# The second memory tile goes from the router's stage into the first pairs of experts, the first one is split, and the results of the memory products are stored once behind the experts

## The chip, the cores and the metric

One Trainium2 chip; the program runs on one of its cores. The metric is the device time of one execution in microseconds (us). TensorE (PE in the rows) has a clock of two levels, 1.2 and 2.4 GHz, and the profile gives the granted mean as a share of the upper one (PEclk).

## The reference

256 tokens (x) of width 1024 go through two blocks. The first adds an attention and mLSTM mix to x, and then a mixture of experts: 32 experts, of which each token uses two of one group. The second block has two layers (GLA and S5), and each layer also reads a memory of 256 rows, `mem_n`, by cross attention. All is in float32.

```python
h2 = modulate(x, norm2_g[l], sh2, sc2)
moe = hier_moe(h2.reshape(b * s, d), w_rg[l], b_rg[l], w_re[l], b_re[l],
               w1[l], w3[l], w2[l]).reshape(b, s, d)
x = x + g2[:, None, :] * moe
...
def memory_attention(q, mem_n, w_kv):
    k, v = jnp.split(mem_n @ w_kv, 2, axis=-1)
```

`mem_n @ w_kv` hangs on nothing in the first block, once the memory is normed. For the GLA layer its weights are four tiles: M0 and M1 give the keys (kept in `kmT`), M2 and a fourth one the values (kept in `vm`). For the S5 layer the keys and values are twelve quarters of a tile and more (`mem_quarters`, 0 to 3 keys, 4 to 11 values), whose results go to a tensor in the chip's memory, `s5_kv`, and are read back near the end.

## The kernel before

The kernel is written engine by engine, with semaphores set by hand. Weights come as tiles of 128 x 4096 floats (2 MB) from SP's queue into a ring of three slots (`k.ring`). The tuple FRONT is the order of the first 24 tiles: tile n goes to slot n % 3, its load waits until tile n - 3 is used (`tile_done`), and TensorE waits until it has landed (`landed`). M means a memory tile, A a tile of the modulation (`w_ada`), O one of the mix's output projection.

Each stage is a block of its own, with a barrier of all engines at its end:

- `stage_mix` ends with O0 and O1; SP loads the tiles up to M1 there, and the first two tiles of expert 0.
- `stage_route` scales x by its norm (`xn`), turns it (`turn`), makes `hT` from it on VectorE (`h_ready`), multiplies by the router's weights, and ranks the tokens of each expert. TensorE's queue holds M1, the turning, A10, the first half of M2 (M20), the router, a row of A10, turning h back, the second half (M21), A11 and the ranks, in this order. SP loads A10, M2, the third tile of expert 0, the first quarter, A11, `norm_f`, and then the three tiles of expert 1, which take the ring's slots as A10, M2 and A11 leave them.
- `stage_experts` works through 16 pairs of experts. The even ones of a pair have three buffers (`expert0`), the odd ones the three ring slots; SP loads each tile for the next pair when TensorE is done with the one in its place. In the first 12 pairs TensorE also multiplies one quarter with the turned memory (`memory_part`); ScalarE copies the result out of PSUM, and issues its store of 128 KB to `s5_kv` on its own queue. SP loads the next quarter between the even and the odd expert's tiles.
- `stage_first_end` adds the experts' sum to x, norms it, and multiplies the fourth memory tile, whose load SP has issued at the experts' end.

The GLA and S5 stages follow; the change does not touch them but for a wait on the ring that goes through `wait_tile`.

Of the kernel before, what the change touches and what calls it, by code (L numbers as in the profile page):

```python
# [15 lines left out]
P = 128  # L16
TOK = 256
TT = TOK // P
D = 1024
KD = D // P  # L20
# [3 lines left out]
RING = 3  # L24
TILE = 4096
# [9 lines left out]
         "O0", "O1", "M1", "A10", "M2", "A11")  # L35
# [11 lines left out]
N_QUARTER = 12  # L47
# [37 lines left out]
class Core:  # L85
# [59 lines left out]
    def wait_tile(self, pe, n):  # L145

        pe.wait_ge(self.landed[n % RING], 16 * (n // RING + 1))
# [108 lines left out]
def half_tile(k, banks, pe, p, kind, src):  # L256
# [3 lines left out]
    pe.wait_ge(*banks.free(p))  # L260
# [13 lines left out]
def ada_tile(k, banks, pe, m, crep):  # L274

    p = f"A{m}"
# [8 lines left out]
    last.then_inc(banks.done(p), 1)  # L285
# [660 lines left out]
def stage_route(k, a):  # L946

    with ExitStack() as ctx:
# [14 lines left out]
        banks = TwoBanks(k, "route", "M10:act M11:act A10:act M20:act G10:dve M21:act A11:act G11:dve")  # L963
# [5 lines left out]
        with k.nc.Block() as block:  # L969
            @block.sync  # L970
            def _(sp):
# [21 lines left out]
            def _(pe):  # L993
                k.wait_tile(pe, TILE_OF["M1"])
                for h in range(2):
                    out = banks.bank(f"M1{h}").rearrange("p (f t) -> p f t", f=2)
                    for f in range(2):
                        for kk in range(KD):
                            last = pe.matmul(out[:, f, :], k.slot(TILE_OF["M1"])[:, kk, (2 * h + f) * P:(2 * h + f + 1) * P],
                                             k.memT[:, kk, :], start=(kk == 0), stop=(kk == KD - 1))  # L1000
                    last.then_inc(banks.done(f"M1{h}"), 1)
# [3 lines left out]
                half_tile(k, banks, pe, "M20", "tm", k.memT)  # L1005
# [13 lines left out]
                half_tile(k, banks, pe, "M21", "tm", k.memT)  # L1019
# [26 lines left out]
            def _(act):  # L1046
# [10 lines left out]
                take("M11", a["kmT"][:, 6:8, :])  # L1057
                take("A10", a["part"][:])
                take("M20", a["vm"][:, 0, 0:512])
# [7 lines left out]
                take("M21", a["vm"][:, 1, 0:512])  # L1067
# [94 lines left out]
def stage_experts(k, a):  # L1162
# [7 lines left out]
    with ExitStack() as ctx:  # L1170
# [29 lines left out]
        with k.nc.Block() as block:  # L1200
            @block.sync
            def _(sp):
# [7 lines left out]
                def load_pair(p, i, off, part):  # L1210

                    for b in range(2):
# [3 lines left out]
                        if part and b == 0:  # L1216
                            sp.wait_ge(part_taken, p * N_QUARTER + i + (off + 1))
                            sp.dma_start(part_w[:].rearrange("p k n -> p (k n)"),
                                         k.dram["mem_quarters"][bass.ds(i + (off + 1), 1)].rearrange("a p n -> (a p) n")
                                         ).then_inc(part_in, 16)  # L1220

                with sp.Fori(0, n_pass) as p:
                    for off, count, part in ((0, N_QUARTER - 1, True), (N_QUARTER - 1, N_PAIR - N_QUARTER, False)):
                        with sp.Fori(0, count) as i:
                            load_pair(p, i, off, part)
                    with sp.If(p < n_pass - 1):
                        sp.dma_start(part_w[:].rearrange("p k n -> p (k n)"), k.dram["mem_quarters"][0]).then_inc(part_in, 16)
# [8 lines left out]
            def _(pe):  # L1236
# [22 lines left out]
                def memory_part(n, part):  # L1259
                    pe.wait_ge(part_in, n * 16)  # L1260
# [1721 lines left out]
```

## Time and profile before

| | before |
|---|---|
| time, median of 3 runs | 1515.02 us (1512.16 to 1519.53) |
| the profiled execution: time | 1515.57 us |
| its span, first to last instruction | 1513.8 us |
| TensorE matmuls busy | 1345.4 us (89%) |
| TensorE weight loads busy | 994.4 us (66%) |
| VectorE busy | 660.8 us (44%) |
| ScalarE busy | 264.6 us (17%) |
| GpSimd busy | 184.2 us (12%) |
| queue of SP, share of 16 DMA engines | 63.2%, 379.78 MB |
| queue of ScalarE | 1.3%, 6.88 MB |

The shares are means over stages with different limits. What a change in one stage is worth is read from that stage: the time line, the waits, and the windows, which give the busy time of each engine and the DMA traffic for a stretch. The route stage runs from 223.5 to about 266 us, the expert stage to about 742 us, and the stage behind it to 761.6 us.

### The profile page before, as it was taken

How to read it: one execution, taken by the hardware profiler on the slowest of the kernel's cores; microseconds unless marked ns; L12 is line 12 of the kernel's file. 1: busy time of each engine (PE TensorE's matmuls, PEld its weight loads, DVE VectorE, ACT ScalarE, POOL GpSimd, SP SyncE). 2: the span in 40 equal slices, each digit the busy share in tenths (PEclk: the TensorE clock that was granted, in tenths of full speed). 3: DMA queues.
4: the chain of work that ended last, by engine and by line, in shares of the span. 5: the costliest groups of instructions: out<-in, count | busy, mean ns of one | idle time of the engine just before them, and what ended most of it. 6: DMA issues, size and time to landing. Idle time of an engine off the chain costs nothing. (4 is left out here: it accounts for less than half of the span.)

```text
span 1513.8 us, 24904 instructions
## 1 busy us (share of the span) xinstructions
PE 1345.4 (89%) x10281; PEld 994.4 (66%) x10281; DVE 660.8 (44%) x1300; ACT 264.6 (17%) x555; POOL 184.2 (12%) x159
## 2 busy tenths in 40 slices
PE   5999989977677867766899999999999999999998
PEld 2475746544455544433458778888878878888887
DVE  2544334211101101110354326366399999886573
ACT  2212101111001100110211022100233323330000
POOL 0000010000000000000157550079300000000000
PEclk9999999998978898898899999999999999999999
DMA  9645737999999999999734334456564444334441
GB/s 401 231 159 224 283 124 319 398 428 428 426 428 428 427 428 428 428 427 429 339 131 167 112 113 165 158 176 227 201 206 160 157 163 137 146 112 152 157 176 45
DMA packets 50104, 387.67 MB, mean 256 GB/s; under 512 B 6368, under 2 KB 21472, under 8 KB 28144
## 3 DMA queue, kind: packets, MB, share of 16 engines
q1 hardware_dynamic: 45712, 379.78, 63.2%
q10 hardware_dynamic: 4320, 6.88, 1.3%
q8 instruction: 51, 0.84, 0.2%
q14 instruction: 21, 0.17, 0.0%
HBM read 379.76 MB, written 6.88 MB: 255 GB/s over the span
## 5 line engine op out<-in xcount | busy, mean ns | idle before, releaser
L2467 PE MATMUL ps<-hT,ring 128*128 128x256 f32 x768 | 174.5, 388 | 1.0 <-PEq L1910 1.0
L2467 PEld LDWEIGHTS ps<-hT,ring 128*128 128x128 f32 x768 | 148.8, 196 | 22.1 <-issue 1.4
L1390 DVE TENSOR_TENSOR act_slots<-gate,ps 64x256 f32<-64x256 f32 x32 | 13.5, 423 | 312.7 <-ACT gate L1337 312.7
L1285 PE MATMUL ps<-expert,x_gathered 128*32 128x256 f32 x1024 | 76.9, 453 | 66.0 <-DMA expert<-in_experts 64.9
L1285 PEld LDWEIGHTS ps<-expert,x_gathered 128*32 128x32 f32 x1024 | 34.6, 124 | 104.0 <-DMA expert<-in_experts 79.6
L1285 PE MATMUL ps<-ring,x_gathered 128*32 128x256 f32 x1024 | 64.8, 405 | 16.9 <-DMA ring<-in_experts 16.9
L1267 PE MATMUL ps<-mem_quarter,memT 128*128 128x128 f32 x256 | 48.2, 375 | 27.0 <-DMA mem_quarter<-in_mem_quarters 27.0
L264 PE MATMUL ps<-ring,hT 128*128 128x512 f32 x160 | 69.8, 593 | 0.0
L1267 PEld LDWEIGHTS ps<-mem_quarter,memT 128*128 128x128 f32 x256 | 46.7, 286 | 33.2 <-DMA mem_quarter<-in_mem_quarters 33.2
L1759 PE MATMUL ps<-ring,zT 128*128 128x256 f32 x288 | 66.8, 379 | 0.0
L1450 POOL TENSOR_SCALAR end_stat<-end_ss 128x1 f32<-128x1 f32 x2 | 0.9, 470 | 519.7 <-ACT expert L1440 519.6
L1285 PEld LDWEIGHTS ps<-ring,x_gathered 128*32 128x32 f32 x1024 | 35.1, 115 | 43.8 <-issue 13.1
L1367 DVE TENSOR_SCALAR sel_weighted<-const,rank,comb 128x128 f32<-128x128 f32 x66 | 19.8, 343 | 90.9 <-PE ps L1250 89.4
L1759 PEld LDWEIGHTS ps<-ring,zT 128*128 128x128 f32 x288 | 54.5, 190 | 7.4
L1953 PE MATMUL ps<-hT,ring 128*128 128x256 f32 x256 | 55.7, 379 | 0.0
L264 PEld LDWEIGHTS ps<-ring,hT 128*128 128x128 f32 x160 | 29.9, 190 | 35.8 <-issue 35.8
L1953 PEld LDWEIGHTS ps<-hT,ring 128*128 128x128 f32 x256 | 48.5, 190 | 6.5
L1255 PE MATMUL ps<-y,selT 32*128 32x256 f32 x528 | 48.4, 438 | 0.5 <-ACT y L1343 0.5
L1813 POOL TENSOR_SCALAR s_out_rstd<-s_out_ss 128x2 f32<-128x2 f32 x1 | 0.4, 368 | 398.5 <-ACT s_out_sq L1806 398.5
L1337 ACT ACTIVATE gate<-ps 64x256 f32<-64x256 f32 x32 | 12.1, 377 | 200.1 <-PE ps L1285 200.1
L283 PE MATMUL ps<-ring,crep 128*32 128x512 f32 x192 | 24.8, 637 | 12.4 <-DMA ring<-in_weights 12.4
L1664 PE MATMUL ps<-ring,hT 128*128 128x256 f32 x144 | 34.5, 382 | 0.0
(651 smaller groups left out, 2486.5 us busy)
## 6 DMA issues: line engine op xcount, KB each, us to landing
ring<-in_weights SPq DMA_DIRECT2D x72, 2048.0 KB, 8.3
expert<-in_experts SPq DMA_DIRECT2D x48, 2048.0 KB, 26.7
ring<-in_experts SPq DMA_DIRECT2D x48, 2048.0 KB, 26.7
mem_quarter<-in_mem_quarters SPq DMA_DIRECT2D x12, 512.0 KB, 20.1
s_c_bar<-c_bar_out ACTq DMA_DIRECT2D x16, 256.0 KB, 2.4
c_bar<-s_c_bar SPq DMA_DIRECT2D x16, 256.0 KB, 2.7
b_raw<-in_s_b SPq DMA_DIRECT2D x16, 128.0 KB, 7.2
s_a_rows<-s_ab_rows SPq DMA_DIRECT2D x64, 32.0 KB, 6.5
```

What stands on the lines that cost most here:

```text
L264: last = pe.matmul(bank, src[:, kk, h * P:(h + 1) * P], w[:, kk, :], start=(kk == 0), stop=(kk == KD - 1))
L283: last = pe.matmul(bank[32 * j:32 * j + 32, :], crep[:, 2 * j + i, :], w[:, 2 * j + i, :], start=(i == 0), stop=(i == 1), skip_group_check ...
L1255: last = pe.matmul(acc(g, t), selT[group(g), b, t * P:(t + 1) * P], y[group(g), :], start=False, stop=stop, skip_group_check=True)
L1267: last = pe.matmul(part_ps[:, h * P:(h + 1) * P], k.memT[:, kk, h * P:(h + 1) * P], part_w[:, kk, :], start=(kk == 0), stop=(kk == KD - 1))
L1285: last = pe.matmul(h_ps[group(g), :], xg[:, f, group(b)], w[:, kk, g, :], start=(f == 0), stop=(f == KD - 1))
L1337: act.activation(gate[:], h_ps[w1_out, :], ACT.Silu).then_inc(silu_done, 1)
L1367: last = dve.tensor_scalar(selw[:, b, t, :], k.c("iota32"), a["rank"][:, t, e], a["comb"][:, t, e], ALU.is_equal, ALU.mult)
L1390: dve.tensor_tensor(act_s[:], gate[:], h_ps[w3_out, :], ALU.mult).then_inc(act_ready, 1)
L1664: last = pe.matmul(self.ps(bank, h), rows[:, kk, :], w[:, kk, :], start=(start and h == 0 and kk == 0), stop=(kk == 3), skip_group_check=True)
L1759: last = pe.matmul(self.sum_of(n, p), rows[:, kk, :], w[:, kk, :], start=(first and kk == 0 and self.PLACE[p][1] == 0), stop=(self.ends(i) ...
L1953: last = pe.matmul(bank[:, f, :], w[:, kk, (2 * h + f) * P:(2 * h + f + 1) * P], k.hT[:, kk, :], start=(kk == 0), stop=(kk == KD - 1))
L2467: last = pe.matmul(out[:, f, :], w[:, kk, (2 * h + f) * P:(2 * h + f + 1) * P], k.hT[:, kk, :], start=(kk == 0), stop=(kk == KD - 1))
```

## The change

M2 leaves the ring. It gets a buffer of its own, `mem_tile`, loaded in the route stage, and is multiplied in four parts of 128 columns in pairs 0 to 3. The quarters move from pairs 0 to 11 to pairs 4 to 15. Their results are copied into `mem_tile`, whose weights are used by then, and one DMA in `stage_first_end` stores all twelve. M1 is multiplied in two halves: the first ahead of the turning, the second in M21's place. In FRONT M1 goes behind A10, and M2 to the end; A11 raises `tile_done` by two in M2's stead.

```diff
-         "O0", "O1", "M1", "A10", "M2", "A11")
+         "O0", "O1", "A10", "M1", "A11", "M2")
...
-        pe.wait_ge(self.landed[n % RING], 16 * (n // RING + 1))
+        outside = TILE_OF["M2"]
+        pe.wait_ge(self.landed[n % RING], 16 * (n // RING + 1 - int(n > outside and n % RING == outside % RING)))
...
-    last.then_inc(banks.done(p), 1)
+    last.then_inc(banks.done(p), 2 if m == 11 else 1)
...
-        banks = TwoBanks(k, "route", "M10:act M11:act A10:act M20:act G10:dve M21:act A11:act G11:dve")
+        banks = TwoBanks(k, "route", "M10:act A10:act G10:dve M11:act A11:act G11:dve")
...
-                tile(TILE_OF["A10"])
-                tile(TILE_OF["M2"])
+                tile(TILE_OF["A11"])
                 load_expert(k, sp, a, 0, 2)
+                sp.dma_start(a["mem_tile"][:], k.dram["weights"][TILE_OF["M2"]]).then_inc(a["mem_tile_in"], 16)
+                at = ROWS["norm_f_g"][0]
+                sp.dma_start(a["norm_f"][:], k.dram["rows"][at:at + D].partition_broadcast(P)).then_inc(norm_f_in, 16)
+                for n in ("A10", "M1", "A11"):
+                    sp.wait_ge(k.tile_done, TILE_OF[n] + 1)
+                    load_expert(k, sp, a, 1, TILE_OF[n] % RING)
                 sp.dma_start(a["mem_quarter"][:].rearrange("p k n -> p (k n)"), k.dram["mem_quarters"][0]
                              ).then_inc(a["mem_quarter_in"], 16)
-                tile(TILE_OF["A11"])
-                at = ROWS["norm_f_g"][0]
-                sp.dma_start(a["norm_f"][:], k.dram["rows"][at:at + D].partition_broadcast(P)).then_inc(norm_f_in, 16)
-                for n in range(T_END_FIRST - RING, T_END_FIRST):
-                    sp.wait_ge(k.tile_done, n + 1)
-                    load_expert(k, sp, a, 1, n % RING)
                 sp.wait_ge(norm_f_in, 16)
...
-        part_out = sb("mem_part", [P, TOK])
-        part_done, part_taken, part_kept = (k.sem(f"mem_part_{x}") for x in ("done", "taken", "kept"))
+        first_w, parts = a["mem_tile"][:].rearrange("p (k n) -> p k n", k=KD), a["mem_tile"][:, 0:N_QUARTER * TOK].rearrange(
+            "p (q m) -> p q m", m=TOK)
+        part_done, part_taken = (k.sem(f"mem_part_{x}") for x in ("done", "taken"))
         part_ps = k.ps[:, 4, 0:TOK]
-        SEGMENTS = ((0, 4, "keys"), (4, 8, "values"), (12, 4, None))
+        SEGMENTS = ((0, 4, "first"), (4, 4, "keys"), (8, 8, "values"))
...
-                    for off, count, part in ((0, N_QUARTER - 1, True), (N_QUARTER - 1, N_PAIR - N_QUARTER, False)):
+                    for off, count, part in ((0, 4, False), (4, N_PAIR - 5, True)):
...
                         for h in range(2):
                             for kk in range(KD):
-                                last = pe.matmul(part_ps[:, h * P:(h + 1) * P], k.memT[:, kk, h * P:(h + 1) * P], part_w[:, kk, :],
+                                w = first_w[:, kk, bass.ds(i * P, P)] if part == "first" else part_w[:, kk, :]
+                                last = pe.matmul(part_ps[:, h * P:(h + 1) * P], k.memT[:, kk, h * P:(h + 1) * P], w,
                                                  start=(kk == 0), stop=(kk == KD - 1))
...
-                                if part and b == 0:
+                                if b == 0:
                                     act.wait_ge(part_done, n)
-                                    act.copy(part_out[:], part_ps).then_inc(part_taken, 1)
-                                    act.wait_ge(part_taken, n)
-                                    act.dma_start(k.dram["s5_kv"][bass.ds(i + off, 1)].rearrange("a p n -> (a p) n"), part_out[:]
-                                                  ).then_inc(part_kept, 16)
-                            if part:
-                                act.wait_ge(part_kept, n * 16)
+                                    if part == "first":
+                                        dst, src = a["vm"][:, :, bass.ds(i * P, P)], part_ps.rearrange("p (h n) -> p h n", h=2)
+                                    else:
+                                        dst, src = parts[:, bass.ds(i + (off - 4), 1), :], part_ps.unsqueeze(1)
+                                    act.copy(dst, src).then_inc(part_taken, 1)
...
+            @block.sync
+            def _(sp):
+                sp.dma_start(k.dram["s5_kv"].rearrange("q p m -> p q m"), a["mem_tile"][:, 0:N_QUARTER * TOK]
+                             .rearrange("p (q m) -> p q m", m=TOK)).then_inc(kept, 16)
+                sp.wait_ge(kept, 16)
```

TensorE's queue in the route stage before, from the stage's start (L992) to the ranks. L999 is M1, L191 the turning of x, L283 a modulation tile (A10, then A11), L264 a half of M2, L1010 the router, L305 a row of A10, L1016 the turning of h:

```order
L992 UNCONDITIONAL_BRANCH
L999 MATMUL ps<-memT,ring 128x256 x32
L191 MATMUL ps<-const,xn1 128x128 x16
L283 MATMUL ps<-ring,crep 32x512 x8
L264 MATMUL ps<-ring,memT 128x512 x8
L1010 MATMUL ps<-w_router,hT 128x36 x16
L305 MATMUL ps<-ada_part,const 128x512
L1016 MATMUL ps<-const,hT 128x128 x16
L264 MATMUL ps<-ring,memT 128x512 x8
L283 MATMUL ps<-ring,crep 32x512 x8
```

The same place of the changed kernel (L271 is a half of M1, L1004 the router):

```order
L994 UNCONDITIONAL_BRANCH
L271 MATMUL ps<-memT,ring 128x256 x16
L192 MATMUL ps<-const,xn1 128x128 x16
L286 MATMUL ps<-ring,crep 32x512 x8
L1004 MATMUL ps<-w_router,hT 128x36 x16
L308 MATMUL ps<-ada_part,const 128x512
L1010 MATMUL ps<-const,hT 128x128 x16
L271 MATMUL ps<-memT,ring 128x256 x16
L286 MATMUL ps<-ring,crep 32x512 x8
```

Ahead of the turning 16 matmuls stand where 32 stood, none stand between A10 and the router, and M1's other half is where M2's second half was.

SP's queue before, from the last tiles of the mix (L376) through the route stage; the barrier between the stages is at L970:

```order
L376 DMA ring<-in_weights 128x4096 [waits tile_done] x3
L370 UNCONDITIONAL_BRANCH [waits late_const_in]
L970 UNCONDITIONAL_BRANCH [waits barrier_Pool_Activation_PE_DVE_SP_release]
L976 DMA w_router<-in_w_router 128x288
L978 DMA b_router<-in_rows 128x36
L974 DMA ring<-in_weights 128x4096 [waits tile_done] x2
L943 DMA expert0_2<-in_experts 128x4096
L982 DMA mem_quarter<-in_mem_quarters 128x1024
L974 DMA ring<-in_weights 128x4096 [waits tile_done]
L986 DMA norm_f<-in_rows 128x1024
L943 DMA ring<-in_experts 128x4096 [waits tile_done] x3
```

SP's queue at the same place of the changed kernel (barrier at L973):

```order
L379 DMA ring<-in_weights 128x4096 [waits tile_done] x4
L373 UNCONDITIONAL_BRANCH [waits late_const_in]
L973 UNCONDITIONAL_BRANCH [waits barrier_Pool_Activation_PE_DVE_SP_release]
L979 DMA w_router<-in_w_router 128x288
L981 DMA b_router<-in_rows 128x36
L977 DMA ring<-in_weights 128x4096 [waits tile_done]
L946 DMA expert0_2<-in_experts 128x4096
L984 DMA mem_tile<-in_weights 128x4096
L986 DMA norm_f<-in_rows 128x1024
L946 DMA ring<-in_experts 128x4096 [waits tile_done] x3
L990 DMA mem_quarter<-in_mem_quarters 128x1024
```

One tile more is loaded in the mix's stage and two ring tiles fewer in the route stage; M2 waits for no slot, and the first quarter stands behind expert 1's tiles.

## Rows read from the trace of the kernel before

**Rows 1.** The page, traffic of the DMA engines in 40 equal slices.

```profile
GB/s 401 231 159 224 283 124 319 398 428 428 426 428 428 427 428 428 428 427 429 339 131 167 112 113 165 158 176 227 201 206 160 157 163 137 146 112 152 157 176 45
```

**Rows 2.** TensorE's waits over the whole span: total us, times, longest.

```profile
PE ps L1285 <- DMA expert<-in_experts: 64.9, 28, 4.2
```

**Rows 3.** Windows from the mix's end to the first block's end.

```profile
core 0: us, PE busy (x) PEld busy (x) DVE busy (x) ACT busy (x) POOL busy (x), PEclk, DMA share, GB/s
...
200.00:224.00 24.00, 20.88 (x62) 10.02 (x61) 7.16 (x12) 0.45 (x1) 0.46 (x2) 1.00 0.00 1
...
254.50:262.00 7.50, 7.50 (x24) 2.95 (x27) 6.66 (x29) 4.56 (x5) 0.00 (x0) 1.00 0.02 5
...
273.00:274.00 1.00, 1.00 (x24) 0.61 (x20) 0.00 (x0) 0.00 (x0) 0.00 (x0) 1.00 0.08 33
...
314.76:593.60 278.84, 208.00 (x2777) 136.18 (x2777) 30.00 (x99) 28.71 (x82) 0.00 (x0) 0.87 1.01 428
624.55:712.63 88.08, 61.11 (x841) 31.35 (x841) 9.72 (x33) 8.27 (x24) 0.00 (x0) 0.84 1.01 428
...
750.00:761.00 11.00, 8.61 (x32) 4.34 (x30) 5.48 (x9) 2.36 (x6) 3.40 (x8) 1.00 0.01 4
```

**Rows 4.** Time line of SP's queue: start, us, what (several issues merged).

```profile
241.29 22.29 SPq L943 DMA_DIRECT2D ring<-in_experts  x3
273.35 9.32 SPq L1208 DMA_DIRECT2D expert<-in_experts  x3
```

**Rows 5.** Time line of TensorE, route stage and first expert.

```profile
223.58 14.05 PE L999 MATMUL ps<-memT,ring 128*128 128x256 f32 x64 [1.80 <-PEq L370]
237.47 1.91 PE L191 MATMUL ps<-const,xn 128*128 128x128 f32 x16
239.31 1.92 PE L283 MATMUL ps<-ring,crep 128*32 128x512 f32 x16
241.16 7.13 PE L264 MATMUL ps<-ring,memT 128*128 128x512 f32 x16
248.13 3.66 PE L1010 MATMUL ps<-w_router,hT 128*128 128x36 f32 x32
...
271.19 1.07 PE L1285 MATMUL ps<-expert,x_gathered 128*32 128x256 f32 x16 [1.09 <-DVE x_gathered L1378]
```

**Rows 6.** Time line of VectorE in the route stage.

```profile
226.90 1.42 DVE L1076 TENSOR_SCALAR xn<-x,x_rstd 128x1024 f32<-128x1024 f32 x2 [3.22 <-POOL x_rstd L184]
...
239.42 3.71 DVE L1079 TENSOR_SCALAR hT<-ps,mod 128x256 f32<-128x256 f32 x8 [11.10 <-PE ps L191]
```

**Rows 7.** VectorE behind O0's end; all loads of L376, their landing.

```profile
214.95 0.69 DVE L935 TENSOR_TENSOR mix_room<-ps,rows_b_g 128x512 f32<-128x512 f32 x1 [1.98 <-PE ps L550]
...
L376 SPq DMA_DIRECT2D ring<-in_weights x21: 327/328/654, 1.7 to 189.1; - x21
...
DMA to landing us min/median/max: 7.6/9.5/19.2
```

**Rows 8.** Time line of TensorE, two memory parts (keys, values).

```profile
274.78 3.72 PE L1263 MATMUL ps<-memT,mem_quarter 128*128 128x256 f32 x16
...
573.73 5.47 PE L1267 MATMUL ps<-mem_quarter,memT 128*128 128x128 f32 x32 [2.73 <-DMA mem_quarter<-in_mem_quarters]
```

**Rows 9.** Time line of TensorE, starts of pairs 2, 11, 12 and 15.

```profile
314.76 3.24 PE L1285 MATMUL ps<-expert,x_gathered 128*32 128x256 f32 x32 [4.21 <-DMA expert<-in_experts]
...
593.60 1.93 PE L1285 MATMUL ps<-expert,x_gathered 128*32 128x256 f32 x32 [2.13 <-DMA expert<-in_experts]
...
624.55 2.43 PE L1285 MATMUL ps<-expert,x_gathered 128*32 128x256 f32 x32 [2.14 <-DMA expert<-in_experts]
...
712.63 1.93 PE L1285 MATMUL ps<-expert,x_gathered 128*32 128x256 f32 x32 [2.67 <-DMA expert<-in_experts]
```

**Rows 10.** Time line of TensorE, starts of the last stage and the next.

```profile
742.67 10.54 PE L1469 MATMUL ps<-ring,memT 128*128 128x512 f32 x24 [0.33 <-PEq L1200]
...
761.61 8.80 PE L1948 MATMUL ps<-ring,hT 128*128 128x512 f32 x16 [2.10 <-PEq L118]
```

More of the change, by code:

```diff
@@ L259, in half_tile @@
     k.wait_tile(pe, n)
-    pe.wait_ge(*banks.free(p))
+    if banks.at[p] >= 2:
+        pe.wait_ge(*banks.free(p))
     w, bank = k.slot(n), banks.bank(p)
@@ L993, in _ @@
             def _(pe):
[L994 to L1001, printed above, removed]
+                half_tile(k, banks, pe, "M10", "fm", k.memT)
                 pe.wait_ge(scaled, TT)
@@ L1018, in _ @@
                 last.then_inc(h_turned, 1)
-                half_tile(k, banks, pe, "M21", "tm", k.memT)
+                half_tile(k, banks, pe, "M11", "fm", k.memT)
                 ada_tile(k, banks, pe, 11, a["crep"])
@@ L1056, in _ @@
                 take("M10", a["kmT"][:, 4:6, :])
-                take("M11", a["kmT"][:, 6:8, :])
                 take("A10", a["part"][:])
-                take("M20", a["vm"][:, 0, 0:512])
                 act.wait_ge(h_turned, 1)
@@ L1066, in _ @@
                 act.copy(a["h2"][:, :, 1, :], rest[:]).then_inc(part_ready, 1)
-                take("M21", a["vm"][:, 1, 0:512])
+                take("M11", a["kmT"][:, 6:8, :])
                 act.wait_ge(*banks.full("G10"))
@@ L1226, in _ @@
                     with sp.If(p < n_pass - 1):
+                        sp.wait_ge(part_taken, p * N_PAIR + N_PAIR)
+                        sp.dma_start(a["mem_tile"][:], k.dram["weights"][TILE_OF["M2"]]).then_inc(a["mem_tile_in"], 16)
                         sp.dma_start(part_w[:].rearrange("p k n -> p (k n)"), k.dram["mem_quarters"][0]).then_inc(part_in, 16)
@@ L1257, in scatter, with memory_part @@
                     return last
-                def memory_part(n, part):
-                    pe.wait_ge(part_in, n * 16)
+                def memory_part(p, i, off, part):
+                    if part == "first":
+                        pe.wait_ge(a["mem_tile_in"], p * 16 + 16)
+                    else:
+                        pe.wait_ge(part_in, p * (16 * N_QUARTER) + (i * 16 + (16 * off - 48)))
                     if part == "keys":
@@ L1271, in pair @@
                 def pair(p, i, off, part):
-                    n = p * N_QUARTER + i + (off + 1)
+                    n = p * N_PAIR + i + (off + 1)
                     for b in range(2):
@@ L1287, in pair @@
                             last.then_inc(done, 1)
-                        if part and b == 0:
-                            memory_part(n, part)
+                        if b == 0:
+                            memory_part(p, i, off, part)
                         pe.wait_ge(sel_ready, s + 1 + b)
                         if b == 1:
-                            if part:
-                                pe.wait_ge(part_taken, n)
+                            pe.wait_ge(part_taken, n)
                             gather()
@@ L1332, in _ @@
                         with act.Fori(0, count) as i:
-                            n = p * N_QUARTER + i + (off + 1)
+                            n = p * N_PAIR + i + (off + 1)
                             for b in range(2):
@@ L1343, in _ @@
                                 act.copy(y[:], y_ps).then_inc(y_ready, 1)
[L1344 removed]
+                                if b == 0:
                                     act.wait_ge(part_done, n)
[L1346 to L1351 removed]
+                                    if part == "first":
+                                        dst, src = a["vm"][:, :, bass.ds(i * P, P)], part_ps.rearrange("p (h n) -> p h n", h=2)
+                                    else:
+                                        dst, src = parts[:, bass.ds(i + (off - 4), 1), :], part_ps.unsqueeze(1)
+                                    act.copy(dst, src).then_inc(part_taken, 1)
             @block.vector
@@ L1408, in stage_first_end @@
                                "vm_half_done", "vm_half_out"))
+        kept = k.sem("s5_kv_kept")
         acc = k.ps[:, 0:4, :].rearrange("p g (t c) -> p t g c", t=TT)
@@ L1533, in sum_weights @@
         t1, t2, t4 = self.weight_sums[i % 2]
-        eng.wait_ge(self.k.landed[n % RING], 16 * (n // RING + 1))
+        self.k.wait_tile(eng, n)
         if i >= self.fresh:
```

8 lines of the change are left out of this document (3 added, 5 removed).

## The prediction

> **What bounds the kernel now.** I read the page first. Of its 40 slices of 37.8 us the ninth to the nineteenth moved 426 to 429 GB/s, and the sixth, just ahead, 124 [rows 1]. The full slices are the expert stage. The list of waits on TensorE says the same: its longest wait in the whole program is for expert tiles, 64.9 us in 28 waits [rows 2]. So the expert stage ends when the last expert tile has landed and been used. Only two things shorten it: fewer bytes in the stream, or a stream that starts earlier. The windows show both. From 314.76 to 593.60 and from 624.55 to 712.63 the DMA share is full at the same 428 GB/s [rows 3], while TensorE has slack (208.0 us busy of 278.84). Ahead of the stream there are two holes: 200 to 224 us, 1 GB/s, and 254.5 to 262 us, 5 GB/s [rows 3].
>
> The second hole has a cause in the order of the work. SP issues the first of the three tiles of expert 1 at 241.29 us and the last at about 263.3 us [rows 4], because each needs a ring slot, and the slots are held by M2 and A11, which TensorE multiplies late. TensorE works through the route stage without a pause: M1 for 14.05 us, turning x, A10, the first half of M2 for 7.13 us, the router [rows 5]. But x is scaled from 226.90 on, in two operations that take 1.42 us together, so ready at 228.3 us, and hT takes 3.71 us from 239.42 on [rows 6]. So x waits 9.1 us for M1's end, and the router waits 5.0 us, from 243.1 to 248.13 us, for the half of M2. The route stage is a chain behind TensorE's own queue, and the memory products stand in it.
>
> **The change, part by part.**
>
> *M1 split, M20 taken out.* Ahead of the turning of x stand 16 matmuls instead of 32: half of 14.05 us, 7.0 us less. x is ready at 228.3 us, and the half ends at 230.6 us, so all of the 7.0 us counts. A10 then ends at 241.2 - 7.0 = 234.2 us, and h_ready comes at 243.1 - 7.0 = 236.1 us. With M20 gone the router starts there, at about 236.3 us instead of 248.13: 11.8 us earlier. Behind it M11 (7.0 us) takes the place of M21 (taken as the 7.13 us of M20), a swap at no cost. VectorE's and ScalarE's chains to the ranks hang on the router's logits and move by the same 11.8 us. The experts' first matmul, 271.19 us before [rows 5], comes at 259.4 us.
>
> *The loads.* SP now loads A10 where M1 stood, as the last issue at 189.1 us [rows 7], and M1 behind O0's end. VectorE adds up O0's second token half at 214.95 us [rows 7], the moment when O0's slot is free, so M1 is issued there, in the 24 us hole. The fastest load of that line lands 7.6 us after its issue [rows 7], so at 222.6 us, 1.0 us before TensorE wants it at 223.58. Of the route stage's loads one tile of 2.1 MB (4.9 us at 428 GB/s) has thus moved into idle time. What is left in the route stage: A11, the third tile of expert 0, M2 into its own buffer, and norm_f, 7.0 MB with the router's weights, 16.4 us, done by about 242 us; then expert 1's tile behind A10 (issued at 234.3, done by 247), and, behind M11 (249.6 us) and A11 (251.5 us), the other two and the first quarter, 4.7 MB or 11.0 us, done by about 261.5 us. The first refill of the expert stage was issued at 273.35 us [rows 4], 2.16 us behind the first expert matmul; now it comes at 261.6 us. The engines are done with the older work by then, so the stream starts 11.8 us earlier: **-11.8 us**. The count of bytes agrees: 4.9 us of it is the tile that is gone from this stretch, the other 6.9 us are holes that shrink.
>
> *The parts in pairs 0 to 3.* Each pair keeps one memory part, but of 16 products over 128 columns (5.47 us) where 8 over 256 columns stood (3.72 us) [rows 8]. That is 1.75 us later for the third tile of expert 0. Before, SP's three issues of that tile row span 273.35 to 282.67 [rows 4]; the first two tiles keep the engines busy for 9.8 us from 274.1, to 283.9 us (in the microsecond behind the issue they still carried only 33 GB/s [rows 3]). The third issue would move from about 282.3 to 284.1 us and reach the engines some 0.8 us later: a hole of about 1.0 us, **+1.0 us**. Later pairs have several tiles queued, so the cost is nothing there. Without that cover it would be 4 x 1.75 = 7.0 us; with a better one, nothing.
>
> *The parts in pairs 12 to 15.* They are new there, 5.5 us of TensorE each. Cover: in the last pair that has one before, TensorE still waits 2.13 us for the next pair's tile at 593.60 [rows 9]. In the last pair of all the next stage's weight tile stands in that place. Cost nothing; if the cover of 2.1 us were gone, some 2 us.
>
> *Stores.* Twelve stores of 128 KB leave the stream. Price from the rows: nine pair periods with quarter and store, (593.60 - 314.76) / 9 = 30.98 us; three with neither, (712.63 - 624.55) / 3 = 29.36 us [rows 9]. The difference is 1.62 us. A quarter of 0.52 MB at 428 GB/s is 1.22 us, so a store costs 0.40 us, and twelve cost **-4.8 us**. By bytes alone (1.57 MB at 428 GB/s) it would be 3.7 us; I take the difference of periods, since it is measured in place. The quarters' loads stay 11 in the stage. The Trainium skill, "Trainium Kernel Development and Optimization", Key Constraints, says that transfers issued from SP, ScalarE and GpSimd all run on the same 16 DMA engines and interleave; a store from ScalarE's queue would be free if that were not so, and by that rule alone moving a load gains nothing unless the engines were idle where it goes. The trace agrees with both halves.
>
> The one store of 1.57 MB comes back behind the experts, on SP. That stage lasts from 742.67 to 761.61 us [rows 10], and from 750 to 761 us the engines carry 4 GB/s [rows 3]. The ring's tiles, ahead of it, are in by 750 us; behind them it needs 12 x 0.40 = 4.8 us and some 2 us to land (7.6 us for a tile of 4.9 [rows 7] leave 2.7 for issue and landing), so it is done by about 757.5 us. Nothing waits but the stage's end. Cost nothing; without the hole 4.8 us.
>
> *The rest* (the ring's rule for the tile outside it, ScalarE writing to SBUF in place of a DMA) is off the path; ScalarE is busy 28.7 us of 278.84 [rows 3].
>
> **Sum.** -11.8 + 1.0 - 4.8 = -15.6 us. The profiled execution took 1515.57 us (its span is 1513.8, with 1.8 around it), so 1499.97; the median of the three is 1515.02, so 1499.4. I say **1500 us**.
>
> **Rivals.** (a) *The stores gave nothing.* The windows with and without them show the same 428 GB/s, so the 0.40 us could belong to the quarters. Then -10.8 us, 1504.7. Against it: a quarter would need 1.62 us for 0.52 MB, 324 GB/s.
>
> (b) *The head start is not kept.* If a tile of expert 1 or M1 came late, or the engines still owed older loads when the stream starts, only the bytes moved into the hole would count: -4.9 + 1.0 - 4.8 = -8.7 us, 1506.9. For it: M1's margin is 1.0 us, and the line's median landing is 9.5 us, 0.9 us too late. Against it: the two late tiles are asked for at 272 us or later.
>
> (c) *The clock, ending slower.* Pairs 0 to 3 and 12 to 15 give TensorE more to do, at a granted clock of 0.84 to 0.87 [rows 3]. If the granted clock stayed at 1.2 GHz through a whole pair, its work would outgrow the loads. Over nine pairs TensorE was busy 208.0 us, 23.1 a pair, at 0.87 [rows 3]: 20.1 us at full clock, 40.2 at 1.2 GHz, 10.8 us above the 29.36 us of the loads. Two such pairs more than before turn the gain into a loss (10.8 x 2 = 21.6), four give 1543 us. Against it: pairs with parts already show 0.87, above the 0.84 of those without. The Trainium skill, "TensorE: Matmul & The Clock Gate", section on HAM oscillation, describes this rule: a loop that does little between waits for DMA is clocked down again and again. By it the route stage's new short waits would cost too.
>
> (d) *No change in effect*, if the route stage hung on something outside TensorE that the trace hides. The back-to-back rows [rows 5] speak against it.
>
> (e) *More*: no hole in pair 0 and a landing that costs less in the last pairs, -17 us or beyond, under 1497.
>
> **How the numbers follow.** Chances: forecast (1497 to 1503) 0.66, (a) 0.11, (b) 0.10, (e) 0.05, (d) 0.04, (c) 0.04. The range 1495 to 1507 takes in the forecast, (a), (b) and most of (e). A measurement of this kernel tells about 0.5%, 7.6 us, from no change: faster means under 1507.4. That holds the forecast, (a), (e) and most of (b), 0.89; same 0.07, slower 0.04.
>
> **What would show it.** Route stage: the router's matmuls at about 236 us, the first expert matmul at about 259.4. Windows: no hole near 255 us but one of 3 to 4 us near 248, a short one in pair 0. Stream: periods of 29.4 us in pairs 2 and 3 and 30.6 from pair 4 on, against 31.0. The stage behind the experts still about 18.9 us long. Wrong if TensorE waits for the ring at the route's start, if the periods stay at 31.0 us, or if the last stage's end waits for the store.

## The result, and the profile after

The changed kernel takes 1502.99 us (median of 5 runs, 1502.14 to 1505.29), the kernel before 1513.83 us in the runs taken with it. The ratio is 0.9922, with a 95% interval of 0.9903 to 0.9941: 10.8 us less by the medians, 9 to 15 us less by the interval, where 15.6 us had been forecast. The profiled execution has a span of 1501.5 us against 1513.8 us, 12.3 us less.

The page first, traffic in 40 slices, to be laid beside [rows 1]:

```profile
GB/s 400 237 132 225 282 202 318 404 426 430 426 428 428 425 429 428 428 427 427 340 176 125 112 165 115 196 182 224 184 189 165 155 165 158 127 112 167 156 174 37
```

The sixth slice rose from 124 to 202 GB/s: M1's tile now crosses in the hole ahead of the route stage. The full slices are as full as before.

TensorE's time line of the route stage, beside [rows 5] (L271 is a half of M1, L192 the turning of x, L286 a modulation tile, L1004 the router, L308 a row, L1010 the turning of h, L1238 the gather, L1284 an expert's tiles, L1266 a memory part):

```profile
225.03 7.14 PE L271 MATMUL ps<-memT,ring 128*128 128x256 f32 x32 [1.80 <-PEq L373]
232.01 1.91 PE L192 MATMUL ps<-const,xn 128*128 128x128 f32 x16
233.85 1.92 PE L286 MATMUL ps<-ring,crep 128*32 128x512 f32 x16
237.72 4.32 PE L1004 MATMUL ps<-w_router,hT 128*128 128x36 f32 x32 [1.95 <-DVE hT L1071]
241.85 2.06 PE L308 MATMUL ps<-ada_part,const 128*128 128x512 f32 x2
243.70 3.62 PE L1010 MATMUL ps<-const,hT 128*128 128x128 f32 x16
247.11 7.30 PE L271 MATMUL ps<-memT,ring 128*128 128x256 f32 x32
...
261.59 2.74 PE L1238 MATMUL ps<-sel,h 128*128 128x64 bf16 x48 [2.61 <-DVE sel_weighted L1364]
265.42 3.66 PE L1284 MATMUL ps<-expert,x_gathered 128*32 128x256 f32 x64 [1.09 <-DVE x_gathered L1375]
269.01 3.84 PE L1266 MATMUL ps<-mem_tile,memT 128*128 x32
```

The reader is to see two things. The router starts 12.69 us behind the stage's start, where it started 24.55 us behind it [rows 5]: 11.86 us are gained there. But the work behind it, the same instructions as before, takes longer: 3.62 us for the turning of h, which is 1.91 us in the trace of before, and 2.06 us for a row of 1.10. The windows say why. Columns as in [rows 3]; first the kernel before, then the changed one:

```profile
248.00:254.00 6.00, 6.00 (x49) 5.34 (x48) 1.80 (x13) 0.60 (x1) 0.00 (x0) 1.00 0.99 418
```

```profile
242.00:248.00 6.00, 6.00 (x23) 4.72 (x23) 4.43 (x31) 0.64 (x1) 0.00 (x0) 0.54 0.99 418
...
250.00:254.00 4.00, 4.00 (x20) 3.54 (x19) 3.62 (x13) 1.90 (x1) 0.00 (x0) 1.00 0.01 4
...
262.00:264.00 2.00, 2.00 (x42) 2.00 (x40) 0.13 (x1) 0.00 (x0) 0.00 (x0) 0.50 0.95 401
```

TensorE's granted clock is 1.00 behind the router's start before, and 0.54 after: it ran almost at the level of 1.2 GHz. It fell behind an idle time of 1.95 us, the wait for `hT`, which the first half of M2 used to fill. It fell again at the gather (0.50), behind the 2.61 us at the barrier. The hole in the traffic, foreseen as 3 to 4 us near 248 us, lasts from about 249 to 255 us: the load that ends it waits for M11, which ends at 254.4 us and was foreseen to end at 249.6.

The spans of the two profiled executions, cut at the same points of the program:

| stretch | before | after | difference |
|---|---|---|---|
| to the route stage's first matmul | 223.58 | 225.03 | +1.45 |
| to the router's first matmul | 24.55 | 12.69 | -11.86 |
| to the memory half behind the turning of h | 6.18 | 9.39 | +3.21 |
| to the first expert matmul | 16.88 | 18.31 | +1.43 |
| expert stage, to the next stage's first matmul | 471.48 | 466.33 | -5.15 |
| the stage behind the experts | 18.94 | 18.86 | -0.08 |
| the rest | 752.19 | 750.89 | -1.30 |

The first and the last row are no work of the change. One modulation tile near the program's start took 3.43 us at 26 us in this execution and 1.92 us before, and the first matmuls behind the experts took 8.80 us before [rows 10] and 7.10 after: the clock's luck, once each way.

In the expert stage, starts of pairs 5, 6 and 15, the last memory part and the stage behind, beside [rows 9] and [rows 10]:

```profile
394.59 3.47 PE L1284 MATMUL ps<-expert,x_gathered 128*32 128x256 f32 x32 [2.68 <-DMA expert<-in_experts]
...
425.24 1.93 PE L1284 MATMUL ps<-expert,x_gathered 128*32 128x256 f32 x32 [0.77 <-DMA expert<-in_experts]
...
701.12 3.29 PE L1284 MATMUL ps<-expert,x_gathered 128*32 128x256 f32 x32 [2.10 <-DMA expert<-in_experts]
...
712.18 5.26 PE L1266 MATMUL ps<-mem_quarter,memT 128*128 128x128 f32 x32 [4.23 <-DMA mem_quarter<-in_mem_quarters]
731.75 10.57 PE L1473 MATMUL ps<-ring,memT 128*128 128x512 f32 x24 [0.41 <-DMA ring<-in_weights]
...
750.61 7.10 PE L1953 MATMUL ps<-ring,hT 128*128 128x512 f32 x16 [2.10 <-PEq L118]
```

Nine periods from 425.24 to 701.12 are 30.65 us each; with a store beside the quarter they were 30.98 us [rows 9]. Pairs 2 to 4 start at 305.65, 335.02 and 364.39 us, 29.37 us apart, without a quarter. So a store took 0.33 us. (The nine periods of before hold one of 31.16 us; pairs 6 to 11 alone, from 438.87 to 593.60 us, are 30.95 us apart, which makes it 0.29 us.) The last pair, now with a memory part, ends when the next weight tile lands, as foreseen. The large store, from the DMA view of the stretch 700 to 760 us:

```profile
s_kv<-mem_tile SPq DMA_DIRECT2D x1, 1536.0 KB, 14.9
```

It was issued at 731.62 us and landed 14.9 us later, at 746.5 us, 4 us ahead of the next stage.

The bytes of the two stretches say what the 5.15 us are. From the DMA view, the expert stage (271.19 to 742.67 us before, 265.42 to 731.75 us after):

```profile
DMA packets 16577, 200.55 MB, mean 425 GB/s; under 512 B 1840, under 2 KB 3376, under 8 KB 4784
```

```profile
DMA packets 14921, 198.32 MB, mean 425 GB/s; under 512 B 1664, under 2 KB 1664, under 8 KB 3200
```

And the stage behind it (742.67 to 761.61 us, and 731.75 to 750.61 us):

```profile
DMA packets 195, 2.67 MB, mean 141 GB/s; under 512 B 32, under 2 KB 32, under 8 KB 32
```

```profile
DMA packets 1789, 4.93 MB, mean 261 GB/s; under 512 B 48, under 2 KB 1584, under 8 KB 1584
```

The expert stage moves 2.23 MB less, 5.2 us at 428 GB/s. The stores are 1.57 MB of it. The other 0.66 MB, 1.5 us, are the end of the next stage's weight tiles: the stage behind the experts moves 2.26 MB more, 1.57 of them the large store, and the remaining 0.69 those tiles.

### The profile page after: what moved, and what is told of

Same layout as the page of the kernel before. It is cut to its first block and busy times, and to the rows that moved or that the text cites. A ratio compares the mean times of both kernels' runs of the same rounds, so it can differ in the third digit from the quotient of the medians.

```text
span 1501.5 us, 25108 instructions
## 1 busy us (share of the span) xinstructions
PE 1338.6 (89%) x10377; PEld 1005.6 (67%) x10377; DVE 660.6 (44%) x1300; ACT 265.1 (18%) x557; POOL 184.1 (12%) x159
## 5 line engine op out<-in xcount | busy, mean ns | idle before, releaser
L1284 PE MATMUL ps<-expert,x_gathered 128*32 128x256 f32 x1024 | 68.8, 416 | 56.0 <-DMA expert<-in_experts 54.9
L1284 PEld LDWEIGHTS ps<-expert,x_gathered 128*32 128x32 f32 x1024 | 32.5, 117 | 91.1 <-DMA expert<-in_experts 69.4
L1266 PE MATMUL ps<-mem_quarter,memT 128*128 128x128 f32 x256 | 49.2, 380 | 34.0 <-DMA mem_quarter<-in_mem_quarters 34.0
L1266 PEld LDWEIGHTS ps<-mem_quarter,memT 128*128 128x128 f32 x256 | 47.7, 292 | 37.8 <-DMA mem_quarter<-in_mem_quarters 37.8
L1284 PE MATMUL ps<-ring,x_gathered 128*32 128x256 f32 x1024 | 59.8, 384 | 7.6 <-DMA ring<-in_experts 7.6
L1284 PEld LDWEIGHTS ps<-ring,x_gathered 128*32 128x32 f32 x1024 | 33.3, 111 | 30.9 <-DMA ring<-in_experts 8.5
L1337 ACT COPY selT<-ps 128x256 f32<-128x256 f32 x32 | 11.9, 373 | 153.8 <-PE ps L1245 153.8
L286 PE MATMUL ps<-ring,crep 128*32 128x512 f32 x192 | 26.3, 671 | 12.5 <-DMA ring<-in_weights 12.5
```

Source lines behind the costliest of these rows:

```text
L286: last = pe.matmul(bank[32 * j:32 * j + 32, :], crep[:, 2 * j + i, :], w[:, 2 * j + i, :], start=(i == 0), stop=(i == 1), skip_group_check ...
L1266: last = pe.matmul(part_ps[:, h * P:(h + 1) * P], k.memT[:, kk, h * P:(h + 1) * P], w, start=(kk == 0), stop=(kk == KD - 1))
L1284: last = pe.matmul(h_ps[group(g), :], xg[:, f, group(b)], w[:, kk, g, :], start=(f == 0), stop=(f == KD - 1))
L1337: act.copy(selT[:, b, :], selT_ps).then_inc(selT_ready, 1)
```

## The experiments

Each was timed against the kernel before on the same chip; the sets of runs come from three chips. "Stretch" is the time from the router's first matmul to the first matmul of the memory half behind it, and "first expert" that from the route stage's first matmul to the first expert matmul. Before they are 6.18 and 47.61 us, in the changed kernel's first profile 9.39 and 40.39 us.

**again.** The changed kernel, profiled once more.

> The changed kernel once more, for a second profile of it. Theory (clock): TensorE's idle 1.95 us before the router lets the granted clock fall, so the stretch from the router's start to the first half's successor (237.72 to 247.11 us in the first profile, 9.39 us) comes out near 9.4 us again, not the 6.2 us that the same work took before. Rival (chance): the fall was this one execution's, as the one at the program's start (26.03 us, 3.43 us for a tile of 1.92) seems to be; then the stretch is 6.2 us here.

1501.49 us, one run. Stretch 11.22 us, first expert 40.82 us. TensorE, the changed kernel's second profile:

```profile
235.47 6.92 PE L1004 MATMUL ps<-w_router,hT 128*128 128x36 f32 x32 [1.95 <-DVE hT L1071]
242.20 2.05 PE L308 MATMUL ps<-ada_part,const 128*128 128x512 f32 x2
244.04 2.81 PE L1010 MATMUL ps<-const,hT 128*128 128x128 f32 x16
```

This time the router itself ran slow, 6.92 us against 3.66 [rows 5]. So the fall is no chance of one execution; only where it starts moves, and with it its length (the first expert's gather ran at full clock here, 1.57 us). The tile near 26 us was quick here (the stage began at 222.78 us): that one is chance.

**fill_route.** TensorE's idle time filled.

```diff
                 ada_tile(k, banks, pe, 10, a["crep"])
+                for _ in range(9):
+                    pe.matmul(k.ps[:, 4, 0:TOK], k.memT[:, 0, 0:P], k.memT[:, 0, :], start=True, stop=True)
                 pe.wait_ge(h_ready, 1)
```

> The changed kernel with nine matmuls of memT by memT (2.0 us, into bank 4, whose content is overwritten) in TensorE's idle time between A10 and the router. Theory (clock): with no idle time the clock stays at 2.4 GHz, the stretch from the router to M11 takes 6.2 us in place of 9.4, the first expert matmul comes 3.2 to 4.6 us earlier against the route stage's start (from 40.4 us down to 36 to 37), and the time is 3 to 4.5 us less than the changed kernel's. Rival (VectorE's or ScalarE's chain sets the stage, TensorE's slower rows are hidden): the stretch shortens but the first expert stays at 40.4 us. Rival (chance): no difference in the stretch.

1500.52 us median, but 1498.48 to 1506.64 over 6 runs; ratio 0.99 (0.9882 to 0.9917). The stretch was 6.18 us, the value of before to the digit, with a clock of 1.00. Each float32 matmul is two passes in the trace, so my filler was twice as long as meant, 4.15 us, and the router started 2.0 us later than in the changed kernel. The first expert came after 38.06 us all the same, 2.3 us earlier than in the changed kernel, though not the 3.2 to 4.6 that were expected. Then the clock fell in another place: in the profiled execution, one of the two longest of the six (1506.64 us), the first expert's tiles ran at half clock, and the first refill's loads, issued behind them, came late. The third was issued some 52 us behind the route stage's start, as in the changed kernel, so nothing of the 2.3 us was left in this one. TensorE's time line and the windows of fill_route:

```profile
239.58 3.66 PE L1006 MATMUL ps<-w_router,hT 128*128 128x36 f32 x32
...
244.01 1.91 PE L1012 MATMUL ps<-const,hT 128*128 128x128 f32 x16
...
262.98 6.07 PE L1286 MATMUL ps<-expert,x_gathered 128*32 128x256 f32 x64 [1.09 <-DVE x_gathered L1377]
```

```profile
239.00:246.00 7.00, 7.00 (x56) 6.37 (x55) 2.20 (x16) 0.04 (x1) 0.00 (x0) 1.00 1.00 426
262.00:268.00 6.00, 5.02 (x48) 2.45 (x52) 1.22 (x3) 0.00 (x0) 0.00 (x0) 0.51 0.72 273
```

**row_first.** A10's row moved into the idle time; no extra work.

```diff
                 ada_tile(k, banks, pe, 10, a["crep"])
+                ada_row(k, banks, pe, 10, a["part"])
                 pe.wait_ge(h_ready, 1)
...
-                ada_row(k, banks, pe, 10, a["part"])
```

> The changed kernel with A10's row (G10, 1.1 us) multiplied ahead of the router's wait instead of behind the router, so that it lies in the idle time. Theory (clock): the idle time falls from 1.95 us to some 0.3 + 0.6 us (wait for ScalarE's copy, then the rest), so the clock may stay up; then TensorE's chain is 1.1 us shorter as well, first expert 4 to 5.7 us earlier against the stage's start, time 3 to 5.5 us less. If short idle times are enough for the fall, the gain is only the 1 us of the row. Rival (chain of VectorE): no more than 1 us in any case.

1498.77 us (1497.84 to 1502.72), ratio 0.9891 (0.9877 to 0.9906). Stretch 6.64 us (5.3 would be full clock without the row), first expert 37.88 us, 2.5 to 2.9 us earlier than in the changed kernel. The clock stayed up through the router and fell in the turning of h (3.25 us).

**m1_whole.** Both halves of M1 ahead of the turning of x.

```diff
-         "O0", "O1", "A10", "M1", "A11", "M2")
+         "O0", "O1", "M1", "A10", "A11", "M2")
...
                 half_tile(k, banks, pe, "M10", "fm", k.memT)
+                half_tile(k, banks, pe, "M11", "fm", k.memT)
...
-                half_tile(k, banks, pe, "M11", "fm", k.memT)
                 ada_tile(k, banks, pe, 11, a["crep"])
```

> The changed kernel with the split undone: both halves of M1 ahead of the turning of x, nothing in M21's old place (M1 loaded ahead of A10 again, the rest as changed). Theory of the prediction (TensorE's queue is the chain): the router starts 7.0 us later; behind it A11 no longer waits for M11 but for VectorE's use of A10's row, 11.9 us behind the router's start by the profile of before. So the first expert comes 5.7 us later than the changed kernel's would at full clock, 1.1 us later than its measured 265.4 us if that held the clock's 4.6 us; time 1 to 6 us more. Rival: the split gave nothing since M11's 7 us only moved from ahead of the router to behind it; then the time is the changed kernel's within 1 us.

1507.57 us (1503.5 to 1514.71, 10 runs), ratio 0.9955 (0.9937 to 0.9973), against 0.9922 for the changed kernel: 4.6 us more by the medians of the two sets. The router started 19.61 us behind the stage's start, 6.9 us later; the first expert came after 44.29 us, 3.9 us later. The clock fell here too, behind the same 1.95 us (from the router to A11 8.05 us, the work of the 6.18 us). The split is worth some 4 us: behind the router part of M11's time is covered, since without it TensorE waits 3.62 us for ScalarE there, and ahead of the router nothing covers it.

**row_fill, fill_both.** row_first with filler, then with a second filler at the head of the expert stage.

```diff
                 ada_tile(k, banks, pe, 10, a["crep"])
+                for _ in range(2):
+                    pe.matmul(k.ps[:, 4, 0:P], k.memT[:, 0, 0:P], k.memT[:, 0, 0:P], start=True, stop=True)
                 ada_row(k, banks, pe, 10, a["part"])
...
                 pe.sem_inc(done, DONE0)
+                for _ in range(2):
+                    pe.matmul(k.ps[:, 4, 0:TOK], k.memT[:, 0, 0:P], k.memT[:, 0, :], start=True, stop=True)
                 pe.wait_ge(sel_ready, 1)
```

> The changed kernel with A10's row ahead of the router's wait and, ahead of the row, two matmuls of memT by memT (128 columns, about 0.7 us, into bank 4, whose content is overwritten), so that TensorE has no idle time between A10 and the router. Theory (clock): the stretch from the router's start to M11's start is at full clock 3.7 + 1.7 = 5.3 us (row_first: 6.64 us, the changed kernel: 9.39 and 11.22 us), and the first expert matmul comes 35.0 to 36.6 us behind the route stage's start (row_first 37.9, fill_route 38.1, changed kernel 40.4 and 40.8), the larger number if the clock falls at the barrier. Time 1 to 2 us under row_first's. Rival (the fall moves on): the clock falls at the next idle stretch instead, the barrier ahead of the experts, and costs there what was saved, as in fill_route, where the first expert's matmuls took 6.07 us in place of 3.66; then the time is row_first's or more.

> row_fill, with two more such matmuls (256 columns, 0.9 us) at the head of the expert stage, inside the 2.61 us in which TensorE waits there for VectorE. Theory (clock): the gather takes 1.57 us and the first two expert tiles 3.66 us, as at full clock; first expert 35.0 us behind the route stage's start; time 0 to 3 us under row_fill's. Rival: the rest of the idle time at the barrier, some 1.5 us, is enough for the fall; no difference to row_fill.

row_fill: 1498.94 us, ratio 0.9889 (0.9868 to 0.9909), stretch 5.38 us, first expert 35.29 us. fill_both: 1498.65 us, ratio 0.9888 (0.9866 to 0.9909), stretch 7.00 us, first expert 36.64 us. In fill_both the clock fell in the turning of h although TensorE had been idle for a quarter of a microsecond only; in row_fill, the same instructions up to there, it did not. The windows of fill_both:

```profile
236.00:238.00 2.00, 1.89 (x18) 1.89 (x17) 0.06 (x1) 0.00 (x0) 0.00 (x0) 1.00 1.00 426
238.00:240.00 2.00, 2.00 (x19) 2.00 (x19) 0.09 (x1) 0.00 (x0) 0.00 (x0) 0.94 1.03 442
240.00:242.00 2.00, 2.00 (x11) 2.00 (x10) 1.63 (x13) 0.00 (x0) 0.00 (x0) 0.50 0.91 383
```

So a fall can come without such an idle time; the router's matmuls of 36 columns ran just ahead of it, but they ran in row_fill too, and what decides between the two is not shown. The second filler showed nothing: the gather took 1.57 us with it and without it. All three variants with the row ahead are the same within their intervals.

**stores_in.** The stores put back into the changed kernel (the large one left out).

```diff
                                     act.copy(dst, src).then_inc(part_taken, 1)
+                                    if part != "first":
+                                        act.wait_ge(part_taken, n)
+                                        act.dma_start(k.dram["s5_kv"][bass.ds(i + (off - 4), 1)].rearrange("a p n -> p a n"), dst
+                                                      ).then_inc(part_kept, 16)
```

> The changed kernel with the twelve stores put back: ScalarE issues one of 128 KB behind each of the twelve copies, in pairs 4 to 15, and the one large store behind the experts is left out. Theory of the prediction (a store takes 0.40 us of the stream): from the first expert matmul to the next stage's start 466.3 + 4.8 = 471.1 us, periods of pairs 5 to 14 at 31.0 us in place of 30.65; time 4 to 5 us more than the changed kernel's. Rival (a), the stores cost nothing: periods 30.65 us, no difference. By what the changed kernel's periods show (30.98 - 30.65 = 0.33 us) it is 4.0 us.

1504.8 us (1500.18 to 1509.66), ratio 0.9931 (0.9905 to 0.9957). Starts of pairs 6 and 15:

```profile
423.93 1.93 PE L1284 MATMUL ps<-expert,x_gathered 128*32 128x256 f32 x32 [0.95 <-DMA expert<-in_experts]
...
702.45 2.17 PE L1284 MATMUL ps<-expert,x_gathered 128*32 128x256 f32 x28 [2.16 <-DMA expert<-in_experts]
```

Nine periods of 30.95 us against 30.65: a store takes 0.29 us, twelve 3.5 us. From the start of pair 2 to the next stage it took 429.56 us against 426.10, 3.5 us more. (Its whole expert stage was 472.3 us, but here the clock had fallen at the first expert, 6.38 us for its tiles.) By the medians it is only 1.8 us more than the changed kernel, where 4 to 5 were expected, and the two intervals overlap: the times alone don't show the stores here, the periods do.

**stores_out.** The stores alone taken out of the kernel before, with a buffer `parts` for the results and the one store behind the experts.

```diff
-                                    act.copy(part_out[:], part_ps).then_inc(part_taken, 1)
...
-                                    act.dma_start(k.dram["s5_kv"][bass.ds(i + off, 1)].rearrange("a p n -> (a p) n"), part_out[:]
-                                                  ).then_inc(part_kept, 16)
+                                    act.copy(a["parts"][:, bass.ds(i + off, 1), :], part_ps.unsqueeze(1)).then_inc(part_taken, 1)
```

> The kernel before with this part of the change alone: the twelve results are kept in a buffer of their own and stored by one DMA behind the experts; the route stage is as before. Theory of the prediction: 4.0 to 4.8 us less than before (1511 against 1515.5), periods with a quarter 30.6 us, the stage behind the experts 18.9 us as before since the store lies in its hole. Rival (a): no difference. Rival (the store at the end is not hidden): the stage behind the experts is up to 4.8 us longer, and nothing is gained.

1512.05 us (12 runs) against 1515.93, 3.9 us less by the medians; ratio 0.9979 (0.9966 to 0.9992), 3.2 us less by the ratio. Pairs 6 to 11 are 30.66 us apart (437.26 to 590.56 us), against 30.95. The expert stage lasts 467.21 us, 4.27 us less than before. The stage behind the experts, time line of stores_out:

```profile
739.42 10.54 PE L1469 MATMUL ps<-ring,memT 128*128 128x512 f32 x24 [0.33 <-PEq L1199]
```

The next stage's first matmul is at 758.36 us, 18.94 us later, as before [rows 10]: the large store is hidden.

**m20_late.** The clock's part shown in the kernel before, by one moved step.

```diff
-                half_tile(k, banks, pe, "M20", "tm", k.memT)
                 pe.wait_ge(h_ready, 1)
...
+                half_tile(k, banks, pe, "M20", "tm", k.memT)
                 half_tile(k, banks, pe, "M21", "tm", k.memT)
```

> The kernel before with one step in another place: the first half of M2 stands ahead of its second half, behind the turning of h, and no longer between A10 and the router. Nothing else changes. Plain queue arithmetic: the router starts 5.0 us earlier (19.6 us behind the route stage's start, not 24.55), the half costs its 7.0 us later, so the first expert comes 2.1 us later than before, 49.7 us behind the stage's start against 47.6, if the clock stays up. Theory (clock): TensorE now idles 1.95 us ahead of the router, and the stretch from the router to the halves takes 9 to 11 us in place of 6.2, so the first expert comes 5 to 7 us later than before, 52.5 to 54.5 us behind the start. Time 5 to 8 us more than before by the theory, 2 by the arithmetic alone.

1522.45 us (12 runs) against 1517.28, ratio 1.0033 (1.0017 to 1.0048). TensorE, m20_late:

```profile
245.72 4.40 PE L1009 MATMUL ps<-w_router,hT 128*128 128x36 f32 x32 [1.95 <-DVE hT L1079]
249.92 2.05 PE L305 MATMUL ps<-ada_part,const 128*128 128x512 f32 x2
251.77 3.62 PE L1015 MATMUL ps<-const,hT 128*128 128x128 f32 x16
255.18 14.04 PE L264 MATMUL ps<-ring,memT 128*128 128x512 f32 x32
```

Its route stage began at 226.12 us, so the router came after 19.60 us, 5.0 us earlier as reckoned; the stretch was 9.46 us, and the first expert came at 280.23 us, after 54.11 us, 6.5 us later than before. Queue arithmetic alone gave 2.1 us. The rest is the clock, without anything else of the change: 3.28 us in the stretch and 1.17 us in the gather (2.74 us against 1.57).

**again_timed, row_first_2.** The changed kernel and row_first on one chip.

> The changed kernel, timed beside row_first on one chip. 1501.5 to 1503 us. If row_first's gain is real (its first expert came 2.5 to 2.9 us earlier in the profiles), this one is 2.5 to 4 us slower than it; the profile is a third one of the changed kernel, and the stretch from the router to M11 should again be 9 to 11 us.

> row_first once more, beside the changed kernel on one chip: 1498 to 1500 us, 2.5 to 4 us under it. The rival (the difference was that of two chips) expects the same time within 1 us.

1502.70 us (1501.22 to 1506.15), ratio 0.9904 (0.9887 to 0.9921), against 1499.09 us (1497.88 to 1502.09), ratio 0.9885 (0.9866 to 0.9904): 3.6 us apart by the medians, in the same direction as before, though the intervals overlap. Over all sets, seven of the nine runs of row_first are shorter than each of the ten of the changed kernel. The changed kernel's stretch was 9.56 us; row_first's was 5.38 us this time, its first expert 35.31 us.

## Why the prediction was right, and where it failed

The forecast was 1500 us, within 1495 to 1507; 1502.99 us was measured. The mechanism was right: an earlier start of the stream, fewer bytes in it, one store in a hole. Three terms were mis-sized, one of them by a step that failed, and the misses partly cancel: the start of the stream came 4.6 us short of its term, the hole in pair 0 was 1.0 us too much, and the expert stage gave 0.35 us more than the term for the stores. That the total is off by only some 3 us is in part luck.

1. **"VectorE's and ScalarE's chains to the ranks hang on the router's logits and move by the same 11.8 us"**, and TensorE's rows behind the router keep their length. This step failed. The router moved by 11.86 us, but the first expert by 7.2 us (47.61 to 40.39). The 4.6 us between are slow TensorE rows, at a granted clock of 0.54 and 0.50. fill_route and row_fill, which fill the idle time, bring the stretch back to full clock; m20_late makes the same fall in the kernel before. The prediction had seen the idle time (A10's end at 234.2, `h_ready` at 236.1) and priced it at nothing, since TensorE only waited there. Rival (c) named the fall, but looked for it in the pairs; its last sentence, that the route stage's new short waits would cost too, came true in all six profiles with that wait (stretches of 9.39, 11.22 and 9.56 us, 7.95 in stores_in, 8.05 in m1_whole, 9.46 in m20_late). The section that it cites (the Trainium skill, "TensorE: Matmul & The Clock Gate", section on HAM oscillation) tells of longer waits for DMA that come again in a loop; here one wait of 1.95 us for VectorE was enough.
2. **The hole in pair 0, +1.0 us**, did not come. The duration of a part with 128 columns was taken from a row at 573.73 us, 5.47 us [rows 8]. At full clock the same work takes 3.84 us, 0.12 us above the part over 256 columns. The row that I took was long because TensorE had waited for data, and its clock had fallen; it does not price the same work in pair 0.
3. **The stores, -4.8 us.** Measured: 0.33 us a store between the two profiles, 0.29 us over like pairs, in stores_in and in stores_out, so 3.5 us. The 0.40 us was a difference of two periods minus a quarter reckoned by its bytes, 1.22 us; the quarter measures 30.65 - 29.37 = 1.28 us, and the 0.06 us went to the store. Bytes alone (3.7 us) were nearer. The expert stage still shrank by 5.15 us, and that the term of 4.8 looks so near is luck. The other 1.5 us are bytes too, but not of stores: 0.66 MB of the next stage's weight tiles, which crossed within the expert stage before and cross behind it now. Before, the stage ended with TensorE's work (30.04 us for the last pair [rows 9, 10], though it had no quarter, with a clock that fell: its second even tile took 3.23 us, now 1.93); now it ends as soon as the first of those tiles has landed (30.63 us with a quarter, which costs 1.28).
4. **M1's margin** held in the profiles: no wait for the ring at the route stage's start in any of them. **The large store** is hidden, by the changed kernel's 18.86 us and by stores_out's 18.94 us. **The parts in pairs 12 to 15** cost nothing. Rival (c) in the pairs did not come: the granted clock over pairs 6 to 14 was 0.89, with every period set by the loads.

-11.86 + 4.64 - 5.15 - 0.08 = -12.45 us, and -12.3 us is the difference of the spans. The 1.45 and 1.30 us of luck at both ends nearly cancel.

A version that beats both kernels exists: row_first, one line moved, 1498.8 and 1499.1 us in two sets of runs. No run here moved the loads of M1 and M2 alone, so what their new places give by themselves is not shown.

## What to carry to other kernels

When a product that only filled time is taken out of TensorE's queue, look at what stays behind: if an idle time of microseconds opens, price the rows behind it at half clock, and look for real work that can stand there, as the row did here. Take a duration from a row only with the granted clock of its window beside it. And where transfers bound a stage, a store moved into a hole behind it pays, by about its bytes at the stage's rate. When a stage's time changes, count its bytes before and after: that tells what left it from what only moved over its end.

## What was not expected of the hardware

The granted clock fell to half level behind 1.95 us of idle time in all six profiles that have it before the router, and stayed there for 3.4 us (m1_whole) to 10 us (again) while TensorE was busy without a break. It also fell in fill_both behind only a quarter of a microsecond of idle time, with the router's 36-column matmuls just ahead, and not in row_fill with the same instructions; and in row_first in one profile and not in the other (turning of h 3.25 and 1.94 us). In the profiles of the kernel before, of stores_out and of fill_route, where TensorE has work right up to the router, it stayed up there. The 2.61 us at the barrier ahead of the experts brought a fall in some executions and none in others: gathers of 1.57 us in the kernel before, and 2.74, 1.57 and 2.74 us in three profiles of the changed kernel.
